# A transformer layer with experts: the joint stage in another order on all engines, and h2 as the start of the expert sums

## The reference

```
m   = sigmoid(g_a) * stick_breaking(x) + sigmoid(g_b) * hgrn2(x)      # the mixer
h2  = layer_norm(ALPHA * x + m @ w_out)                               # ALPHA = 2 ** 0.25
s   = sigmoid(h2 @ w_router); sb = s + router_bias
# group score = sum of its two largest sb; the best 4 of 8 groups stay; then the best 8 of 64 experts by sb
w   = s[chosen] / sum(s[chosen]) * 2.5
ffn = sum_e w_e * (silu(h2 @ Wg_e) * (h2 @ Wu_e)) @ Wd_e  +  (silu(h2 @ w_sg) * (h2 @ w_su)) @ w_sd
out = layer_norm(ALPHA * h2 + ffn)
```

## Time and profile before

| | |
|---|---|
| median of 3 runs | 2580.18 us (2578.97 to 2580.81) |
| the profiled execution | 2570.26 us |
| its span in the trace | 2568.5 us |
| mean granted clock of PE | 0.973 of full speed |
| busy: PE, DVE, ACT, POOL | 2354.5, 1545.5, 1049.4, 1449.4 us |
| joint stage, experts, last stage | about 1440 to 1683, to 2508, to the end |

### The profile page before, as it was taken

One profiled execution on the slowest core, in us unless ns is written; L12 is line 12 of the kernel. 1 busy time (PEld: TensorE's weight loads), 2 busy tenths in 40 slices (PEclk: granted clock), 3 DMA queues, 4 the chain that ended last, 5 costly groups with the idle time before them and its releaser, 6 DMA issues. The chain is left out here.

```text
span 2568.5 us, 38247 instructions
## 1 busy us (share of the span) xinstructions
PE 2354.5 (92%) x14242; PEld 2118.0 (82%) x14242; DVE 1545.5 (60%) x2665; ACT 1049.4 (41%) x1726; POOL 1449.4 (56%) x1519
## 2 busy tenths in 40 slices
PE   4999999999999999999989699979999999999980
PEld 4889899898898998988969476569999999989870
DVE  7375775756757758567577587744444454445335
ACT  3442624525436245264363232213444444444332
POOL 6354664665646546555466335666666676776530
PEclk9999999999999999999999799989999999999995
DMA  5201111011111110111111431469999999999995
GB/s 181 66 23 42 47 35 55 26 43 47 35 34 47 44 47 26 43 47 35 34 46 67 149 99 58 143 189 293 324 323 334 341 343 346 344 347 354 360 343 168
DMA packets 210708, 380.67 MB, mean 148 GB/s; under 512 B 25794, under 2 KB 132670, under 8 KB 210010
## 3 DMA queue, kind: packets, MB, share of 16 engines
q1 hardware_dynamic: 180330, 302.31, 33.5%
q0 software_dynamic: 28960, 71.44, 11.1%
q10 hardware_dynamic: 1232, 4.46, 0.5%
HBM read 315.23 MB, written 71.95 MB: 151 GB/s over the span
## 5 line engine op out<-in xcount | busy, mean ns | idle before, releaser
L124 PE MATMUL ps<-xTh,w_mix_low 128*128 128x368 f32 (+1 forms) x1728 | 594.8, 344 | 10.2 <-POOL w_mix_low L118 8.9
L125 PE MATMUL ps<-xTl,w_mix_high 128*128 128x368 f32 (+1 forms) x1728 | 569.0, 329 | 0.0
L126 PE MATMUL ps<-xTh,w_mix_high 128*128 128x368 f32 (+1 forms) x1728 | 566.6, 328 | 0.0
L2054 POOL DMA_INDIRECT xg_early<-h_d,tabq_early x310 | 320.0, 1032 | 110.6 <-issue 90.3
L124 PEld LDWEIGHTS ps<-xTh,w_mix_low 128*128 128x128 f32 x1728 | 325.5, 188 | 21.9 <-issue 18.6
L125 PEld LDWEIGHTS ps<-xTl,w_mix_high 128*128 128x128 f32 x1728 | 325.6, 188 | 9.1 <-issue 6.3
L126 PEld LDWEIGHTS ps<-xTh,w_mix_high 128*128 128x128 f32 x1728 | 325.3, 188 | 0.0
L2066 POOL DMA_INDIRECT ys_d<-yo,tab_early x114 | 211.6, 1856 | 179.8 <-DMA ys_d<-yo,tab_early 127.5
L1277 POOL TENSOR_TENSOR x_m<-x_m,kh_m 128x128 f32<-128x128 f32 (+1 forms) x272 | 127.8, 470 | 218.3 <-ACT x_m L830 218.3
L118 DVE TENSOR_TENSOR wdl<-wd_early,wdh 128x2048 fp32r<-128x2048 f32 x64 | 146.7, 2292 | 133.4 <-ACT wdh L113 133.4
L118 POOL TENSOR_TENSOR w_mix_low<-w_mix_raw,w_mix_high 128x1024 fp32r<-128x1024 f32 x72 | 174.9, 2429 | 88.6 <-ACT w_mix_high L113 88.3
(11 more groups left out here) (361 smaller groups left out, 5001.0 us busy)
## 6 DMA issues: line engine op xcount, KB each, us to landing
wd_early<-in_w_exp_down SPq DMA_DIRECT2D x64, 1024.0 KB, 12.4
wg_early<-in_w_exp_gate SPq DMA_DIRECT2D x82, 512.0 KB, 6.2
wu_early<-in_w_exp_up SPq DMA_DIRECT2D x82, 512.0 KB, 12.0
w_mix_raw<-in_w_in SPq DMA_DIRECT2D x72, 512.0 KB, 3.8
wg<-in_w_exp_gate SPq DMA_DIRECT2D x42, 512.0 KB, 7.0
wu<-in_w_exp_up SPq DMA_DIRECT2D x42, 512.0 KB, 11.9
xg_early<-h_d,tabq_early POOLq DMA_INDIRECT x316, 6.8
mT_d<-gs_m SPq DMA_DIRECT2D x8, 544.0 KB, 2.7
```

Source lines behind the costliest of these rows:

```text
L124: pe.matmul(out, ll, rh, start=start, stop=False)
L125: pe.matmul(out, lh, rl, start=False, stop=False)
L126: return pe.matmul(out, lh, rh, start=False, stop=stop)
L2054: pool.indirect_dma_start(out=xg[:, b, g, :], out_offset=None, in_=h2_d[:, :].rearrange("t (q n) -> (t q) n", q=4), in_offset=bass.Indirec ...
```

## The change

It does the following.

- **Order.** The queues of PE, DVE, ACT and POOL in the joint stage are new lists. `gate_up(n)` becomes `gate(n)` and `up(n)`, `shared(t)` becomes `shared(t, b)`, `sums(t)` becomes two `half(t, b)` and `spread(t)`, so that halves stand between other work. On ACT, `high(t + 3)` stands ahead of `evacuate(t)`. On POOL, `send(t)` stands ahead of later shifts.
- **Route and slots.** The groups are chosen with the engine's search for eight largest and a replacement in place of a table of comparisons. A token's choices are taken in order of expert number ("sorted places"): a key `expert * KEYS + slot + 1` for the chosen, zero for others, and one search for the eight largest gives place and expert together.
- **h2 as beginning of the sums.** SP stores h2 in `ys_d` too. ACT scales the shared rows by 1/ALPHA, POOL adds them to `ys_d` with an accumulating transfer (`add_shared`), and the gates are divided by ALPHA. The last layer norm then needs `ys_d` alone, with its epsilon divided by ALPHA squared.
- **The last norm** moves into the block of the experts (`last_norm`), ahead of `overflow`, which does it again if it had work. SP waits for the adds itself. The loads of h2 (`xr`, nine) at the end of the experts go. Tiles 1 and 4 are measured on DVE, the others on ACT.

The rest of the diff, cut to its core:

```diff
-                sp.dma_start(h2_d[t * P:t * P + m, :], y[:m, t % 2, :]).then_inc(stored[t % 2], 16)
+                for rows_d in (h2_d, ys_d):
+                    sp.dma_start(rows_d[t * P:t * P + m, :], y[:m, t % 2, :]).then_inc(stored[t % 2], 16)
...
+            def half_hidden(n, wt, bank, done):
                 f, ci = gu[n]
                 c0, cw = CHUNKS[ci]
+                for k in range(KT):
+                    mm = pe.matmul(ps[:, bank, 0:cw], wt[:, k, f * P:(f + 1) * P], xT[:, k, c0:c0 + cw], start=k == 0, stop=k == KT - 1)
+                mm.then_inc(done, 1)
+
+            def gate(n):
+                f, ci = gu[n]
                 if n == 0:
                     pe.wait_ge(w_in, 48)
                 if f == 0:
-                    pe.wait_ge(h_copied, 2 * -(-(c0 + cw) // P))
-                downs = [d for d in range(len(down)) if plan_of_downs[d] <= n]
-                if downs:
-                    e = downs[-1]
-                    pe.wait_ge(y_left, e // 2 + 1)
-                    pe.wait_ge(y_right, e // 2 + 1)
-                for wt, bank, done in ((wg, G, g_done), (wu, U, u_done)):
-                    if n:
-                        pe.wait_ge(*((sl_done, n) if bank == G else (h_done, n)))
-                    for k in range(KT):
-                        mm = pe.matmul(ps[:, bank, 0:cw], wt[:, k, f * P:(f + 1) * P], xT[:, k, c0:c0 + cw],
-                                       start=k == 0, stop=k == KT - 1)
-                    mm.then_inc(done, 1)
-
-            plan_of_downs = {2 * t + b: at for t, at in ((0, 2), (1, 2), (2, 4), (3, 4), (4, 4), (5, 6), (6, 6), (7, 6), (8, 6))
-                             for b in range(2)}
-
-            def shared(t):
+                    pe.wait_ge(h_copied, 2 * -(-sum(CHUNKS[ci]) // P))
+                if n >= 4:
+                    pe.wait_ge(y_left, n - 3)
+                elif n:
+                    pe.wait_ge(sl_done, n)
+                half_hidden(n, wg, G, g_done)
+
+            def up(n):
+                if n >= 4:
+                    pe.wait_ge(y_right, n - 3)
+                elif n:
+                    pe.wait_ge(h_done, n)
+                half_hidden(n, wu, U, u_done)
+
...
+            def shared(t, b):
                 m = rows(t)
-                pe.wait_ge(h_done, plan_of_downs[2 * t])
-                for b in range(2):
-                    if t:
-                        pe.wait_ge((y_left, y_right)[b], t)
-                    if b == 0:
-                        pe.wait_ge(sl_done, plan_of_downs[2 * t])
-                    for f in range(2):
-                        mm = pe.matmul(ps[:m, (G, U)[b], :], hT[:, f, t * P:t * P + m], wd[:, f, cols(b)], start=f == 0, stop=f == 1)
-                    mm.then_inc(d_done, 1)
-
...
-                own, other = gs[:m, :].unsqueeze(2).to_broadcast(B), gs[:m, :].unsqueeze(1).to_broadcast(B)
-
-                ch(dve.tensor_tensor(cmp_[:m, 0, :, :], other, own, ALU.is_gt))
-                ch(dve.tensor_tensor(cmp_[:m, 1, :, :], other, own, ALU.is_equal))
-                ch(dve.tensor_tensor(cmp_[:m, 1, :, :], cmp_[:m, 1, :, :], earlier[:m, :, :], ALU.mult))
-                ch(dve.tensor_tensor(cmp_[:m, 0, :, :], cmp_[:m, 0, :, :], cmp_[:m, 1, :, :], ALU.add))
-                ch(dve.tensor_reduce(rank[:m, 0, :], cmp_[:m, 0, :, :], AX.X, ALU.add))
-                ch(dve.tensor_scalar(rank[:m, 1, :], rank[:m, 0, :], float(TOPG), None, ALU.is_lt))
-                ch(dve.tensor_scalar(rank[:m, 2, :], rank[:m, 1, :], -1.0, -NEG_BIG, ALU.add, ALU.mult))
+                ch(dve.max(last_key[:m, :], gs[:m, :]))
+                ch(dve.tensor_copy(best[:m, 0:TOPG], last_key[:m, 0:TOPG]))
+                ch(dve.match_replace(left[:m, :], best[:m, :], gs[:m, :], 4 * NEG_BIG))
+                ch(dve.tensor_scalar(barred[:m, :], left[:m, :], 2 * NEG_BIG, -2 * NEG_BIG, ALU.is_lt, ALU.mult))
                 v3 = sbm[:m, :].rearrange("p (g e) -> p g e", g=NGRP)
-                ch(dve.tensor_tensor(v3, v3, rank[:m, 1, :].unsqueeze(2).to_broadcast([m, NGRP, EPG]), ALU.mult))
-                ch(dve.tensor_tensor(v3, v3, rank[:m, 2, :].unsqueeze(2).to_broadcast([m, NGRP, EPG]), ALU.add))
+                ch(dve.scalar_tensor_tensor(out=v3, in0=barred[:m, :].unsqueeze(2).to_broadcast([m, NGRP, EPG]), scalar=NEG_BIG, in1=v3,
+                                            op0=ALU.add, op1=ALU.min))
                 ch(dve.max(top[:m, :], sbm[:m, :]))
-                ch(dve.max_index(picks[:m, t, :], top[:m, :], sbm[:m, :]))
...
-                mm = dve.tensor_scalar(gates[:m, t, :], gates[:m, t, :], tot[:m, 1:2], ROUTE_SCALE, ALU.mult, ALU.mult)
+                mm = dve.tensor_scalar(gates[:m, t, :], gates[:m, t, :], tot[:m, 1:2], ROUTE_SCALE / ALPHA, ALU.mult, ALU.mult)
...
-                ch(dve.tensor_tensor(slot[:m, :], slot[:m, :], BASE[:m, :], ALU.add))
-                ch(dve.tensor_copy(pf[:m, :], picks[:m, t, :]))
-                ch(dve.tensor_tensor(hot[:m, :, :], NUM[:m, :].unsqueeze(1).to_broadcast(B),
+                ch(dve.tensor_tensor(slot[:m, :], slot[:m, :], key_base[:m, :], ALU.add))
+                ch(dve.tensor_tensor(slot[:m, :], slot[:m, :], chosen[:m, t, :], ALU.mult))
+                ch(dve.max(last_key[:m, :], slot[:m, :]))
+                ch(dve.max_index(picks[:m, t, :], last_key[:m, :], slot[:m, :]))
+                ch(dve.tensor_scalar(pf[:m, :], picks[:m, t, :], float(CAP - KEYS), -1.0, ALU.mult, ALU.add))
+                ch(dve.tensor_tensor(dest[:m, t, :], pf[:m, :], last_key[:m, :], ALU.add))
+                ch(dve.tensor_tensor(hot[:m, :, :], code[:m, :].unsqueeze(1).to_broadcast(B),
                                      pf[:m, :].unsqueeze(2).to_broadcast(B), ALU.is_equal))
-                ch(dve.tensor_tensor(prod[:m, :, :], hot[:m, :, :], slot[:m, :].unsqueeze(1).to_broadcast(B), ALU.mult))
-                ch(dve.tensor_reduce(df[:m, :], prod[:m, :, :], AX.X, ALU.add))
-                ch(dve.tensor_copy(dest[:m, t, :], df[:m, :]))
...
+                act.activation(ys[:m, t % 2, cols(b)], ps[:m, (G, U)[b], :], ACT.Copy, scale=1.0 / ALPHA).then_inc((y_left, y_right)[b], 1)
...
-            def store(t):
-                m = rows(t)
-                act.wait_ge(y_left, t + 1)
-                act.wait_ge(y_right, t + 1)
-                act.dma_start(ys_d[t * P:t * P + m, :], ys[:m, t % 2, :]).then_inc(y_out[t % 2], 16)
...
+            def add_shared(t):
+                m = rows(t)
+                pool.wait_ge(y_left, t + 1)
+                pool.wait_ge(y_right, t + 1)
+                pool.wait_ge(stored[t % 2], 32 * (t // 2 + 1))
+                pool.dma_start(ys_d[t * P:t * P + m, :], ys[:m, t % 2, :], accum_op=ALU.add).then_inc(y_out[t % 2], 16)
...
-            for t in range(NT):
-                m = rows(t)
-                sp.dma_start(xr[:m, t, :], h2_d[t * P:t * P + m, :]).then_inc(ahead_in, 16)
-            sp.dma_start(gcol[:, :], a["ln2_g"][0].partition_broadcast(P)).then_inc(ahead_in, 16)
-            sp.dma_start(bcol[:, :], a["ln2_b"][0].partition_broadcast(P)).then_inc(ahead_in, 16)
-            sp.wait_ge(ahead_in, 16 * (NT + 2))
...
+    def _(sp):
+        sp.dma_start(gcol[:, :], a["ln2_g"][0].partition_broadcast(P)).then_inc(rows_in, 16)
+        sp.dma_start(bcol[:, :], a["ln2_b"][0].partition_broadcast(P)).then_inc(rows_in, 16)
+        for rows_added, count in added:
+            sp.wait_ge(rows_added, count)
+        for t in range(NT):
+            m = rows(t)
+            sp.dma_start(xr[:m, t, :], ys_d[t * P:t * P + m, :]).then_inc(y_in[t], 16)
+        for t in range(NT):
+            m = rows(t)
+            sp.wait_ge(y_ready, t + 1)
+            dst = o[0][0, t * P:t * P + m, :] if t < NT - 1 else o[1][0, :, :]
+            sp.dma_start(dst, xr[:m, t, :]).then_inc(stored, 16)
+        sp.wait_ge(stored, 16 * NT)
...
+        def measure(t):
+            n = BY_VECTOR.index(t)
+            m = rows(t)
+            dve.wait_ge(y_in[t], 16)
+            for c in range(2):
+                dve.bn_stats(parts[:m, 6 * c:6 * c + 6], xr[:m, t, 512 * c:512 * c + 512]).then_inc(moment, 1)
+            dve.wait_ge(moment, 2 * n + 2)
+            dve.bn_aggr(norm[:m, 8 + n, 0:2], parts[:m, 0:12]).then_inc(moments, 1)
...
+        dve.wait_ge(rows_in, 32)
+        for t in range(NT):
+            if t + 1 in BY_VECTOR:
+                measure(t + 1)
+            finish(t)
...
+            act.activation(dump, xr[:m, t, :], ACT.Copy, accum_out=total[:m, col]).then_inc(summed, 1)
+            act.wait_ge(summed, n + 1)
+            act.activation(mean[:m, col], total[:m, col], ACT.Copy, scale=-1.0 / D).then_inc(centre, 1)
+            act.wait_ge(centre, n + 1)
+            act.activation(dump, xr[:m, t, :], ACT.Square, bias=mean[:m, col], accum_out=spread[:m, col]).then_inc(spread_ready, 1)
+            act.wait_ge(spread_ready, n + 1)
```

(52 more changed lines are left out.)

507 lines of the change are left out of this document (288 added, 219 removed).

## The result

| | before | after |
|---|---|---|
| median of 7 runs each | 2578.69 us (2577.58 to 2580.81) | 2587.51 us (2582.19 to 2591.33) |
| the profiled execution, its span | 2570.26, 2568.5 us | 2591.0, 2588.0 us |

The ratio after to before is 1.0031, with a 95% interval of 1.002 to 1.0042. The forecast was 2568, the range ended at 2582, and "slower" had 0.13. The two profiled executions lie further apart (20.7 us) than the medians (8.8): the one before lies 7.3 us under the lowest of its seven runs, the one after 3.5 us over its median. What follows splits the 20.7, and the experiments are judged by medians.

A forecast was written before the change was run, and what follows sets the result against it. PE and what it waits for were taken to set the joint stage's pace. From the profiled 2570.26 us, +3.3 (joint stage) and -15.1 (last stage) gave 2558.5; 11.8 off the median 2580.18 gave 2568, range 2546 to 2582.

The forecast's parts named there:

- the four cycles: Joint stage: four turns from the end of shift(0) at 1466, 68.2 us together, put shift(4) at 1534.2.
- behind `shift(8)`: Joint stage's end: shorter work after shift(8) at 1640.3, PE last, tables at 1686.2, first gather at 1687.0.
- the last stage: After the experts: norm starts 10.7 us sooner, runs 7.4 shorter, closing work takes back 3: -15.1 us.
- the cycle from shift to shift: Joint stage, one shift's end to the next, through stores, mT load, high, root and scaling: 16.4 us, 17.7 with table load.
- rival C: POOL's queue: sends ahead of shifts delay shift(8) past 1657, so the kernel is slower, 2586 to 2595 us; chance 0.13.
- `shift(4)` to `shift(8)`: Joint stage: sends on POOL and slots on DVE set the pace, from 1534.2 to 1640.3.
- none after 1641: Sign on PE in the new trace: waits of 3 to 5 us for h_copied and y_ready, none after 1641.
- the 3 us for the closing work: Kernel's end: the plan's read and branch, worth between nothing and 7.7 us, taken as 3.
- B: Joint stage: loads of mT don't bind, shift(8) at 1617, 20 us gained, 2545, between 2540 and 2560; chance 0.25.
- E: Experts' start: the accumulating stores disturb it, 2575 to 2584 us; chance 0.05.
- The hold: Joint stage: POOL's instructions block DVE through the shared port; sums include 2.1 us, 2.1 and 5 as holds.
- up to 20 us: Joint stage: addition by the shared-port rule if all 17 shifts and splits, in place of six, were held against DVE.

The follow-up runs named there:

- e5: The changed kernel with m_load(t + 3) in place of m_load(t + 2), ahead of SP's wait for y_ready, and m_load(2) ahead of the loop: 2546.52 us.
- e9: The changed kernel with idle products, read by nobody, in four of PE's waits in the first five tiles: 2577.02 us.
- e7: The changed kernel with POOL's sends put behind the shifts, the load of mT still late: 2592.19 us.
- e8: The changed kernel with POOL's sends behind the shifts and the load of mT ahead of SP's wait for y_ready: 2562.15 us.

## Why the prediction was wrong, point by point

The profiled execution was forecast at 2558.5 us and took 2591.0. The 32.5 between them are: 5.3 at the start and the first tile, 9.8 in the four cycles to `shift(4)`, 0.7 from there to `shift(8)`, 10.1 behind `shift(8)`, 4.4 at the hand-over, 2.1 in the experts' stretch and 0.1 in the last stage. The median missed by less, 19.5, and that is luck: the forecast added the 9.9 us by which the profiled execution before lay under its median, and the one after lies 3.5 over its own.

**The step that failed** is the cycle from shift to shift, "from the end of one shift to the end of the next: stores 3.1, issue 0.35, `mT` 5.7 ... 16.4 us, or 17.7 with the table", and with it the path behind `shift(8)`, below, which had no wait in it. The mechanism of the cycle was right: ACT waits for `mT`, and e5 shows that this wait is the whole difference between a slower kernel and a much faster one. Its size was off, in three ways.

- From the end of a shift to the issue of `x_load` it took 4.0, 5.5, 4.0 and 6.9 us in the four cycles, against 3.45 in the sum: 6.6 us of the 9.8 that are missing. In the first and third cycle the stores land last, 4.0 us behind the shift, and by e9 they would in all four: about 2.1 of the 6.6 are stores that were taken too short. The other 4.5 are `turn(t)` in the second and fourth cycle, which PE reaches only behind a project half. That term was not in the sum at all. The second cycle, from the end of `shift(1)` at 1489.02 (SP, PE, SP):

```profile
1489.05 0.32 SPq L1449 DMA_DIRECT2D h_d<-y  x1
...
1493.44 1.03 PE L1496 MATMUL ps<-ident,y 128*128 128x128 f32 x8
...
1494.56 0.32 SPq L1429 DMA_DIRECT2D y<-xn_d  x1
```

- The fall of the clock behind PE's waits is what made these turns late. The prediction named it, as something that could make rival C worse, and costed it at nothing. e9, with the clock up, has no cycle above 4.0, ends `shift(4)` 6.1 us sooner and is 9.9 us better.
- In the third cycle `low(5)` and `shift(3)` stood behind `send(0)`: DVE was done at 1522.7, POOL began `shift(3)` at 1525.85, 3.1 us later.

The four cycles measured 78.0 us against 68.2. `shift(4)` to `shift(8)` measured 106.8 against 106.1: the part of the sum that went along the queues of POOL and DVE was right, step by step too (32.6, 23.9, 23.5 and 26.9 us where it had 31.1, 24.2, 23.0 and 27.8).

**Behind `shift(8)`** 46.7 us were forecast and 56.8 measured. PE was in `up(3)` when `shift(8)` ended, with a shared half still ahead of `turn(8)`, which started 3.2 us later; it then waited 0.45, 0.79, 1.33 and 2.20 us where "none after 1641" was forecast, a shared half ran at the slow clock (3.50 for 1.72), and a later half waited 0.51 for the landing of a store. These make up the 10.1. The longer waits for such landings, 4.83 and 2.89, come behind the first gather, at the hand-over. A ledger of one engine with no wait in it is a lower bound.

**The first tile and the start** were 5.3 us later than forecast, 3.1 of them before the stage.

**The last stage** was right: -15.1 forecast, -15.0 measured. The last add went 0.27 us behind the last `yo`, its landing took 6.3, and SP's loads went at once. The norm's first data came 10.5 us behind the last `yo` (21.2 before, 10.7 sooner as forecast), and from there to DVE's last result it took 27.4 us (27.3 forecast, though its parts of 23.1, 3.4 and 0.6 add up to 27.1). From that result to the end of the execution, with what lies around the span, it was 8.7 us, 5.8 before: the 3 us for the closing work hold too.

**The rivals.** B was right in mechanism, for another kernel: with the load out of the way `shift(8)` ends at 1618.1 (it said 1617). That the time, 2546.5, also meets its 2545 is in part luck: the first gather came 53.5 us behind `shift(8)` where B had 46, so 12.0 us sooner than before and not 20, and between profiled executions e5 gains 23.5 us, not 35. What B had wrong for this kernel was that the queue as written would have the load there in time. Where the slower case was put, C's mechanism is refuted by e7 and e8. The measured 2587.5 lies in C's range (2586 to 2595), and its condition (`shift(8)` after 1657) was missed by only 0.9 us, but both through late loads and a low clock instead. E's place was real and small: 4.4 us at the hand-over. An accumulating store costs POOL 0.86 to 1.05 us of issue (1.6 was taken); the cost was the wait for its landing.

**The hold** did not add up to the 20 us of the whole rule. Beside POOL's arithmetic and its memset ten DVE instructions of the stage took longer than elsewhere, 10.6 us in all, about what the sum had. On DVE's timeline, while `shift(2)` ran on POOL (1505.96 to 1508.31):

```profile
1506.52 0.69 DVE L1673 BATCH_NORM_STATS2 st<-y 128x6 f32<-128x512 f32 x1
...
1507.50 0.22 DVE L1731 TENSOR_TENSOR slot<-slot,ps 128x64 f32<-128x64 f32 x1
1507.76 0.63 DVE L1733 TENSOR_TENSOR slot<-slot,key_base 128x64 f32<-128x64 f32 x1
```

Statistics with one operand, and an addition with one operand in PSUM, ran through at their usual length; the addition of two tensors in SBUF was held, to 1508.39. Another kind was held as well, the scaling of a tile (0.81 us elsewhere), while `low(3)` ran on POOL from 1482.42 to 1484.77:

```profile
1483.64 1.68 DVE L1685 TENSOR_SCALAR y<-y,st 128x1024 f32<-128x1024 f32 x1
```

The section of the Trainium skill that the prediction cited, "SBUF: two separate sides" in "SBUF — State Buffer", limits the rule to DVE instructions with two inputs in SBUF, against a POOL instruction that reads SBUF, and to those in a mode that uses two ports; the prediction had left that out when it came to "up to 20 us". The trace agrees on the first kind, and does not show the mode of the second.

**What stays open** is why the change's loss is 20.7 us between two profiled executions and 8.8 between medians, and how e9's 9.9 us come about, of which its profiled execution shows 6.1 at `shift(4)`, 4.8 at the first gather and 6.7 at the end. Of the kernel before there is one trace, so where its other runs are 7 to 11 us slower than that one can't be seen.

## What to carry to other kernels

When an order is written anew so that an engine asks for a buffer one tile earlier, the queue that fills the buffer has to be moved by a tile too: look for every wait and every earlier transfer that stands ahead of that load in its own queue, and for what releases each. The reordered kernel was 8.8 us slower than before with the load where it was, and 32.4 faster with one index changed. A cycle is costed by walking that queue with all its waits, here `turn` on PE beside the stores. A stage in which PE begins to wait should be costed with its products at the slow clock for some microseconds behind each wait: here the granted clock fell behind all four waits of 2.7 to 5.5 us.

## What the runs showed of the hardware

- Four waits of PE filled with 60 idle products made the kernel 9.9 us faster than the change (both against before), though none of their results was used: the granted clock of 1480 to 1490 us went from 0.66 to 1.00.
- A store of 512 KB issued by POOL took 13.34 us to land as an accumulating one (DMA share 1.00 from 1707 to 1720) and 11.90 as a plain one (0.73 from 1706 to 1718); plain stores of the same size by SP took 2.7 us in the median (`h_d<-y`), at a share of 0.44 from 1440 to 1560.
- Accumulating stores keep the DMA engines busier for fewer bytes: share 0.84 at 118 GB/s, where plain ones had 0.43 at 176 GB/s.
- Beside a POOL addition of two SBUF tensors, the DVE instructions with two SBUF operands were held (0.63 and, beside `shift(5)`, 1.77 us in place of 0.22). Beside POOL's subtraction so was a scaling of 128x1024 with one (1.36 and 1.68 in place of 0.81). Beside POOL's memset an addition with two ran at its usual 0.23, and a scaling of 128x64 was held (1.44 in place of 0.25).
